# First stage of a hybrid mLSTM / RG-LRU / MoE step: token tiles in single file, loads of SP in one order, constants on ScalarE's queue

## The reference

```python
xs = x_sample + grid_pos_embed(x_sample.shape[1], D_MODEL)[None]        # latent tokens only
mod_ctx = (silu(c_ctx) @ w_ada[l] + b_ada[l]).reshape(1, N_MOD, D_MODEL)
mod_lat = (silu(c) @ w_ada[l] + b_ada[l]).reshape(bs, N_MOD, D_MODEL)
sh1, sc1, g1, sh2, sc2, g2 = [mod[:, j][:, None, :] for j in range(N_MOD)]
hn = rmsnorm(x, lp['norm1']) * (1 + sc1) + sh1
z = (hn @ lp['w_in'])      # q, k, v, o, gates (16 columns), xr, gr
```

## Time and profile before

| | |
|---|---|
| median of 3 runs | 2114.51 us (2108.32 to 2136.52) |
| profiled execution, its own time | 2117.95 us |
| its span | 2116.2 us |
| first stage, from the start to the first work of the next | about 90 us |
| TensorE's mean granted clock | 0.967 of full |

### The profile page before, as it was taken

One profiled execution on the slowest core, in us unless ns is written; L12 is line 12 of the kernel. 1 busy time (PEld: TensorE's weight loads), 2 busy tenths in 40 slices (PEclk: granted clock), 3 DMA queues, 4 the chain that ended last, 5 costly groups with the idle time before them and its releaser, 6 DMA issues. The chain is left out here.

```text
span 2116.2 us, 31750 instructions
## 1 busy us (share of the span) xinstructions
PE 1920.4 (91%) x8869; PEld 1342.3 (63%) x8870; DVE 1268.5 (60%) x1853; ACT 1072.9 (51%) x1530; POOL 740.4 (35%) x761
## 2 busy tenths in 40 slices
PE   4787998999998997699999999999999999999980
PEld 2344444999896454566777766767767777676660
DVE  3376447432778699675666555555665666555556
ACT  3354545442234111556666656566666666666652
POOL 4211000000013044443556444346656653335350
PEclk9899999999999998799999999999999999999995
DMA  8732200332104224337967897866677888887854
GB/s 262 237 134 102 67 21 20 120 120 71 11 1 175 90 90 150 140 135 261 321 170 225 305 324 244 298 181 171 165 252 253 273 275 283 279 295 250 283 141 178
DMA packets 119099, 390.10 MB, mean 184 GB/s; under 512 B 28541, under 2 KB 53117, under 8 KB 94077
## 3 DMA queue, kind: packets, MB, share of 16 engines
q1 hardware_dynamic: 72908, 271.53, 35.0%
q0 software_dynamic: 45840, 117.76, 21.7%
q10 hardware_dynamic: 290, 0.02, 0.0%
HBM read 347.08 MB, written 80.41 MB: 202 GB/s over the span
## 5 line engine op out<-in xcount | busy, mean ns | idle before, releaser
L2083 DVE TENSOR_TENSOR wupl<-big,wuph 128x2048 fp32r<-128x2048 f32 x234 | 525.8, 2289 | 462.0 <-ACT wuph L2021 398.7
L2021 ACT ACTIVATE wuph<-big 128x2048 fp32r (+1 forms) x234 | 435.8, 1917 | 13.0 <-issue 8.5
L1946 PE MATMUL bank<-w,hT 128*128 (+1 forms) x920 | 414.0, 593 | 0.3 <-issue 0.3
L1925 PE MATMUL bank<-wuph,xTh 128*128 128x512 f32 x928 | 372.2, 401 | 12.1 <-DVE xTl L2092 11.5
L1925 PE MATMUL bank<-wuph,xTl 128*128 128x512 f32 x928 | 364.6, 393 | 0.0
L1925 PE MATMUL bank<-wupl,xTh 128*128 128x512 f32 x928 | 363.4, 392 | 0.0
L1859 POOL DMA_INDIRECT yacc_scratch<-y,idx_s x106 | 213.3, 2012 | 422.3 <-issue 381.5
L1946 PEld LDWEIGHTS bank<-w,hT 128*128 128x128 f32 x920 | 166.0, 190 | 165.6 <-issue 165.6
L2011 ACT ACTIVATE y<-bank 128x512 f32<-128x512 f32 x115 | 68.8, 598 | 296.6 <-PE bank L1946 227.0
L1925 PEld LDWEIGHTS bank<-wuph,xTh 128*128 128x128 f32 x928 | 175.8, 189 | 49.4 <-issue 15.9
L1925 PEld LDWEIGHTS bank<-wuph,xTl 128*128 128x128 f32 x928 | 174.6, 188 | 37.1
(11 more groups left out here) (358 smaller groups left out, 2690.3 us busy)
## 6 DMA issues: line engine op xcount, KB each, us to landing
big<-in_exp_w SPq DMA_DIRECT2D x128, 1024.0 KB
w<-in_exp_w SPq DMA_DIRECT2D x64, 1024.0 KB
wada<-in_w_ada POOLq DMA_DIRECT2D x16, 1024.0 KB, 6.2
wg<-in_w_in SPq DMA_DIRECT2D x14, 1024.0 KB, 5.4
wada<-in_w_ada SPq DMA_DIRECT2D x4, 2048.0 KB, 11.5
big<-in_w_in SPq DMA_DIRECT2D x8, 1024.0 KB, 5.4
x<-x_scratch SPq DMA_DIRECT2D x9, 512.0 KB
x_scratch<-x SPq DMA_DIRECT2D x9, 512.0 KB, 2.6
```

Source lines behind the costliest of these rows:

```text
L1925: mm = pe.matmul(b_up[j][:, :], x[:, k, :], w[:, :, k, :], start=(k == 0 and i == 0), stop=(k == KT - 1 and i == 2))
L1946: mm = pe.matmul(b_down[half][:, :], hT[:, i, :], w2[:, at, i, half * 512:(half + 1) * 512].rearrange("p s n -> p (s n)"), start=(i == 0), ...
L2021: act.activation(part13(wup[j][0], half), raw13(e % WSLOT, half), ACT.Copy).then_inc(w_high, 1)
L2083: dve.tensor_tensor(part13(wup[j][1], half), raw13(e % WSLOT, half), part13(wup[j][0], half).bitcast(F32), ALU.subtract).then_inc(w_low, 1)
```

## The change

The tile groups stay, but only as the groups of the load semaphores. The work goes tile by tile: ACT takes a root for each tile (`root(t)`, two tiles ahead of the turn), DVE a reciprocal for each tile inside `norm(t)`, and DVE's loop does `position(t + 2)` and then `norm(t)`. PE does `position(t + 3)` behind `turn(t)`. The sequence of turns and blocks is now 0, 1, block 0, 2, 3, 4, block 1, 5, 6, block 2, 7, 8, block 3. SP issues tiles and blocks in one list, `LOADS`. POOL keeps the tables, the small loads and the stores; `cst` moves to ACT's queue.

```diff
--- before.py
+++ after.py
@@ -221,7 +221,7 @@
         ss, rs = sb("ss1", [P, NT]), sb("rs1", [P, NT])
         s_ada = [sem(f"ld_ada{j}") for j in range(NA)]
         s_bada, s_x1, s_pos = sem("ld_bada"), sem("st_x1"), sem("ld_pos")
-        s_x = [sem(f"ld_x{j}") for j in range(NG)]
+        s_x = [sem(f"ld_x{j}") for j in range(4)]
         pick_set, pos_in, gate_sums = (sem(n) for n in ("pick_set", "pos_in", "gate_sums"))
         s_cc, s_cst, bd_zero = sem("ld_cc"), sem("ld_consts"), sem("bd_zeroed")
         ring_banks, pos_banks, gate_bank, col_banks = m.banks[0:4], m.banks[6:8], m.banks[4], [m.banks[5], m.banks[7]]
@@ -236,14 +236,15 @@
         small = small_loads(a, m)
         m.ld_all = 16 * (len(small) - 1)
 
-        TAKE = [[0, 1], [2, 3], [4, 5], [6, 7, 8]]
-        group = {t: g for g, tiles in enumerate(TAKE) for t in tiles}
         MODS = [0, 2, 1, 3]
         BY_ACT, BY_DVE = (0, 1, 4), (2, 3, 5, 6, 7)
-        seq = ([("turn", t) for t in TAKE[0]] + [("mod", 0)] + [("turn", t) for t in TAKE[1]] + [("mod", 1)] +
-               [("turn", t) for t in TAKE[2] + TAKE[3]] + [("mod", 2), ("mod", 3)])
-        AHEAD = {("start", 0): [1, 2], ("turn", 1): [3], ("mod", 0): [4], ("turn", 3): [5], ("mod", 1): [6], ("turn", 5): [7, 8]}
-        COLUMNS = {("turn", 3): [0], ("turn", 6): [1], ("mod", 3): [2, 3]}
+        GROUP = [[0, 1], [2, 3], [4, 5], [6, 7, 8]]
+        group = {t: g for g, tiles in enumerate(GROUP) for t in tiles}
+        LOADS = [("x", 0), ("x", 1), ("mod", 0), ("x", 2), ("x", 3), ("mod", 1), ("x", 4), ("x", 5), ("mod", 2), ("x", 6), ("x", 7),
+                 ("x", 8), ("mod", 3)]
+        seq = ([("turn", t) for t in (0, 1)] + [("mod", 0)] + [("turn", t) for t in (2, 3, 4)] + [("mod", 1)] +
+               [("turn", t) for t in (5, 6)] + [("mod", 2)] + [("turn", t) for t in (7, 8)] + [("mod", 3)])
+        COLUMNS = {("turn", 5): [0], ("turn", 6): [1], ("mod", 3): [2, 3]}
         jobs_before, n = {}, 0
         for item in seq:
             jobs_before[item] = n
@@ -255,7 +256,11 @@
 
         @block.sync
         def _(sp):
-            for j in range(NG):
+            for kind, j in LOADS:
+                if kind == "x":
+                    src = a["x_prompt"][0] if j == 0 else a["x_sample"][0, (j - 1) * P:j * P, :]
+                    sp.dma_start(x[j][:, :], src).then_inc(s_x[group[j]], 16)
+                    continue
                 if j >= NA:
                     sp.wait_ge(full, jobs_before["mod", j - NA] + 1)
                 g = MODS[j]
@@ -278,13 +283,9 @@
             pool.dma_start(posr, a["pos_row"]).then_inc(s_pos, 16)
             for b in range(2):
                 pool.dma_start(posc[64 * b:64 * b + 64, :], a["pos_col"]).then_inc(s_pos, 16)
-            for t in range(NT):
-                src = a["x_prompt"][0] if t == 0 else a["x_sample"][0, (t - 1) * P:t * P, :]
-                pool.dma_start(x[t][:, :], src).then_inc(s_x[group[t]], 16)
-                for dst, src in small[3 * t:3 * t + 3]:
-                    pool.dma_start(dst, src, allow_slow_non_contiguous=True).then_inc(s_cst if dst is small[0][0] else m.ld, 16)
-                if t == 0:
-                    pool.memset(m.bd[:, :, :, :, :], 0.0).then_inc(bd_zero, 1)
+            for dst, src in small[1:]:
+                pool.dma_start(dst, src, allow_slow_non_contiguous=True).then_inc(m.ld, 16)
+            pool.memset(m.bd[:, :, :, :, :], 0.0).then_inc(bd_zero, 1)
             pool.wait_ge(full, total - 1)
             for t in range(NT):
                 pool.wait_ge(x_pos, t + 1)
@@ -335,7 +336,7 @@
 
             pe.wait_ge(pick_set, 1)
             pe.wait_ge(s_pos, 48)
-            for t in AHEAD["start", 0]:
+            for t in (1, 2):
                 position(t)
             pe.wait_ge(silu_c, 1)
             pe.wait_ge(s_bada, 16)
@@ -344,8 +345,8 @@
                     modulation(t)
                 else:
                     turn(t)
-                for tt in AHEAD.get((kind, t), ()):
-                    position(tt)
+                    if t + 3 < NT:
+                        position(t + 3)
                 for j in COLUMNS.get((kind, t), ()):
                     columns(j)
 
@@ -365,20 +366,20 @@
             ring = Ring(act, ring_banks, full, free)
             act.dma_start(m.cc[:, 0, :], a["c_ctx"].rearrange("(p k) -> p k", k=KT)).then_inc(s_cc, 16)
             act.dma_start(m.cc[:, 1, :], a["c"][0].rearrange("(p k) -> p k", k=KT)).then_inc(s_cc, 16)
+            act.dma_start(small[0][0], small[0][1]).then_inc(s_cst, 16)
             act.dma_start(bada[:, :], a["b_ada"][:, 0:NG * 512]).then_inc(s_bada, 16)
             act.wait_ge(s_cc, 32)
             act.activation(cct[:, :, :], m.cc[:, :, :], ACT.Exp, scale=-1.0).then_inc(e_cc, 1)
             act.wait_ge(s_cst, 16)
 
-            def squares(g):
-                for t in TAKE[g]:
-                    act.wait_ge(x_pos, t + 1)
-                    if t >= 1:
-                        act.wait_ge(x_sq, t)
-                    act.activation(sq, x[t][:, :], ACT.Square, accum_out=ss[:, t:t + 1]).then_inc(x_sq, 1)
-                c = slice(TAKE[g][0], TAKE[g][-1] + 1)
-                act.wait_ge(x_sq, TAKE[g][-1] + 1)
-                act.activation(rs[:, c], ss[:, c], ACT.Sqrt, scale=1.0 / D, bias=m.epsc).then_inc(x_root, 1)
+            def root(t):
+
+                act.wait_ge(x_pos, t + 1)
+                if t >= 1:
+                    act.wait_ge(x_sq, t)
+                act.activation(sq, x[t][:, :], ACT.Square, accum_out=ss[:, t:t + 1]).then_inc(x_sq, 1)
+                act.wait_ge(x_sq, t + 1)
+                act.activation(rs[:, t:t + 1], ss[:, t:t + 1], ACT.Sqrt, scale=1.0 / D, bias=m.epsc).then_inc(x_root, 1)
 
             def modulate(k):
 
@@ -387,6 +388,8 @@
                                          scale=sc_col[:, k, s:s + 1], bias=sh_col[:, k, s:s + 1])
                 ins.then_inc(done_act, 1)
 
+            root(0)
+            root(1)
             for kind, t in seq:
                 if kind == "mod":
                     bank = ring.drain()
@@ -394,8 +397,8 @@
                     act.wait_ge(mod_row, t + 1)
                     ring.drained(act.activation(mrow[t][:, 256:512], bank[32:34, 0:256], ACT.Copy))
                 else:
-                    if t == TAKE[group[t]][0]:
-                        squares(group[t])
+                    if t + 2 < NT:
+                        root(t + 2)
                     for half in range(2):
                         bank = ring.drain()
                         ring.drained(act.activation(m.hnT[:, 4 * half:4 * half + 4, t * P:(t + 1) * P],
@@ -425,7 +428,7 @@
                             m.ident[0:16, 0:16].unsqueeze(2).to_broadcast([16, 16, 64])).then_inc(pick_set, 1)
 
             def position(t):
-                dve.wait_ge(s_x[group[t]], 16 * len(TAKE[group[t]]))
+                dve.wait_ge(s_x[group[t]], 16 * len(GROUP[group[t]]))
                 if t == 0:
                     dve.sem_inc(x_pos, 1)
                     return
@@ -436,6 +439,8 @@
                 dve.tensor_tensor(x[t][:, 512:1024], x[t][:, 512:1024], posc, ALU.add).then_inc(x_pos, 1)
 
             def norm(t):
+                dve.wait_ge(x_root, t + 1)
+                link(dve.reciprocal(rs[:, t:t + 1], rs[:, t:t + 1]))
                 if t >= 2:
                     dve.wait_ge(full, jobs_before["turn", t - 2] + 2)
                 dve.tensor_scalar(hn[t % 2][:, :], x[t][:, :], rs[:, t:t + 1], None, ALU.mult).then_inc(x_hn, 1)
@@ -457,14 +462,12 @@
                                             ALU.mult, ALU.add)
                 ins.then_inc(done_dve, 1)
 
-            for g, tiles in enumerate(TAKE):
-                for t in tiles:
-                    position(t)
-                c = slice(tiles[0], tiles[-1] + 1)
-                dve.wait_ge(x_root, g + 1)
-                link(dve.reciprocal(rs[:, c], rs[:, c]))
-                for t in tiles:
-                    norm(t)
+            position(0)
+            position(1)
+            for t in range(NT):
+                if t + 2 < NT:
+                    position(t + 2)
+                norm(t)
             dve.wait_ge(m.ld, m.ld_all)
             for half in range(2):
                 modulation_columns(half)
```

## The result

The changed kernel takes 2122.94 us (median of 20 runs, 2118.93 to 2136.5), the kernel before 2113.09 (20 runs, 2106.98 to 2136.52). The ratio is 1.0049, 95% interval 1.0035 to 1.0063: **about 10 us slower**, far inside 2% and clear of the noise: the interval is 0.14% to either side, much finer than the 2% that the prediction named as the limit. The forecast was a loss of 1.4 us.

What follows compares the result with a forecast made beforehand. It took the first stage's end to be paced by tile 3's landing, block 0 and tile 8's landing; 75.8 - 74.4 = +1.4 us makes the profiled 2117.95 into 2119.4, forecast median 2116, range 2103 to 2134.

Steps and rivals of the forecast that it cites:

- A, the landing of tile 3: First loads of the first stage: tile 3 lands at 19.3 us, at 316 GB/s, bounds 18.8 to 29.0.
- A to the end of block 0: DVE and PE waiting for each other from tile 3's landing at 19.3; block 0 ends at 34.2.
- Block 0 to B: Block 2 and tiles 6 to 8, issued from 34.3 behind block 0; tile 8 lands at 47.8.
- B to the end of block 3: From tile 8's landing at 47.8: block 1 ends at 57.3, block 2 at 68.9, block 3 at 75.8.
- DVE's scaling of tile 0: On DVE behind the position of tile 2, so waiting for tiles 2 and 3; done at 21.7.
- the earlier constants: Constants on ACT's queue land at 9 to 10 instead of 15.5; six us won, nothing comes of them.
- the 16.0 us at the end: Fixed chain from the last block's end to the next stage's first matmul, 16.0 us, untouched by the change.
- The first turn: PE's first turn in the stage, claimed near 22 and not 24.4.
- The wait for tiles 6 to 8: DVE idle about 8 us before adding tile 6, from near 40 to 47.8, released by a transfer.
- the one on the slow side: Rival: SP's queue no faster than before, first loads until 29.0, block 3 ends at 85.5, +11 us, 2126; chance 0.12.
- Faster transfers: Rival: data sooner than the rates, tile 3 at 17, four transfers in 11.5; -2.9 us, 2112; chance 0.22.
- That rival: ScalarE changes tables for each root: up to 22 us more on ACT, time near 2130; chance 0.01.

Runs made afterwards that it cites:

- the two halves of the change: Two kernels against the kernel before: new loads with the old group order, ratio 0.9987; new tile-by-tile order with the old loads, ratio 1.0035.
- Small late: The changed kernel with POOL's small loads behind the landing of tiles 2 and 3; ratio 1.0007 to the kernel before.
- tiles ahead: The changed kernel with tiles 6 to 8 requested ahead of block 2; ratio 1.0022 to the kernel before.
- groups, same loads: Old group order with new loads, tiles 6 to 8 ahead of block 2, small loads behind tiles 2 and 3; ratio 0.9989 to the kernel before.
- loads only: The new SP load list and constants on ACT's queue, with the old group order; ratio 0.9987 to the kernel before.
- added matmuls: The changed kernel with extra PE matmuls, results unused, where PE waits; ratio 1.0046 to the kernel before.
- all three repairs: The changed kernel with scaling before next position, tiles 6 to 8 ahead of block 2, small loads behind tiles 2 and 3; 2099.86 us, ratio 0.9911 to the kernel before.
- before, small late: The kernel before with POOL requesting its small loads behind the requests of the nine tiles; ratio 1.0000 to the kernel before.

## Why the prediction was right in kind and wrong in size

The order of events was right, the size was not: 1.4 us were forecast and 11.05 are in the trace, 9.8 in the medians. The range held it because it was 31 us wide, mostly for the spread of few runs. And a forecast of 1.4 us hardly has a sign: it was the rest of gains and losses several times as large (7.7 us lost and 3.8 won in the two halves of the change), so that its sign came out is partly luck. Two terms failed, the rate of the first loads and the price of PE's work behind a wait. Step by step, each difference of 85.45 - 75.8 = 9.65 us has its place:

- **A, the landing of tile 3: 23.3 instead of 19.3, +4.0.** The term failed by its rate. I took 316 GB/s from a stretch in which POOL's list spread the small loads between 512 KB tiles. The change bunches them ahead of A, and the rate to 23 us was 246. *Small late* shows it: A came at 17.35. I had counted the small loads by their bytes, 0.1 MB, and they cost 6 us here.
- **A to the end of block 0: 19.7 instead of 14.9, +4.8.** The step's chain was right (turn, position, addition, scaling, each behind the other), its prices were not: turns 1.94 and 1.97 for 1.73, positions twice 2.07 for 1.12, block 0 7.0 for 4.15, in all 5.2. The prices came from a PE that had just done two turns in a row; the change gives it one turn and then a wait. The durations are those that PE has at the lower level of its clock from 50 to 60 us, though the column does not show the level here (last section). I named the clock only as something outside the stage.
- **Block 0 to B: 12.65 instead of 13.6, -0.95.** The four transfers were issued and landed as priced:

```profile
wada<-in_w_ada SPq DMA_DIRECT2D x1, 2048.0 KB, 8.6
yT<-in_x_sample SPq DMA_DIRECT2D x3, 512.0 KB, 10.0
```

  From the issue to the last landing they took 12.6 us. The rows gave 13.5, and the fit of the Trainium skill ("DMA: Bandwidth & Descriptors", Anatomy of one DMA) gave an estimate of 10.4. The page states this fit for transfers issued from GpSimd, and these are SP's; the measurement is nearer to the rows.
- **B to the end of block 3: 29.8 instead of 28.0, +1.8.** Again the durations: block 1 took 6.0 us, turn 4 1.97, position 7 2.07, and the loss is 2.75 at the end of block 1. Behind it 0.96 came back, because turn 5 took 1.10 for 1.73 and turns 7 and 8 1.97 for 2.68.

The steps on the order held. DVE's scaling of tile 0 waited for tiles 2 and 3; the earlier constants, 5.2 us and not six, were worth nothing, since tile 1's position was done at 15.04 and DVE then stood idle for the 8.26 us; DVE was idle for 8 us before tile 6 and tile 4's scaling stood right behind; the 16.0 us at the end did not move. The first turn, forecast near 22, began at 25.73, later than the 24.38 before. The wait for tiles 6 to 8 was put on the path with its full length, and *tiles ahead* shows that half of it was.

Of the rivals, the one on the slow side named +11 us and 2126, near the measured time, but its mechanism did not happen: it wanted A at 29.0, and A came at 23.3. Of the 9.65 us that the forecast missed, 4.0 are its kind of delay. *Faster transfers* was wrong as the change stood; with the small loads out of the way it came true (330 GB/s, A at 17.35). ScalarE loaded its table for the roots once, at 11.64, and never again in the stage. (That rival's price was off too: 22 us on top of 2116 make 2138, not 2130.) What I had not listed as a rival, PE's longer durations inside the stage, is the largest single miss, 5.2 us up to block 0 alone.

## What to carry to other kernels

When a loop is changed from groups to single items, look at what stands ahead of each step on its engine: "prepare t+2, then finish t" makes the finished item wait for the load of a later one, and swapping the two was worth 15.9 us of a 75 us stage. Price a PE step that will follow a wait at the longer duration that the trace shows behind a wait, not at the one it had in a run of work. Count small strided loads by their packets, and put them behind what is awaited, but expect a gain only where the tiles are what is waited for: it was 6.8 us in the changed kernel and nothing in the kernel before. And a transfer that is moved behind another one inherits that one's wait.

## What was not expected of the hardware

- Matmuls of one form have two durations in this stage, 1.12 and 2.07 for a position, 1.10 and 1.97 for a turn of eight, 3.62 and up to 6.48 for a block. The granted clock of two stretches of the changed kernel (busy us and count of PE, PEld, DVE, ACT and POOL, then the granted clock, the DMA share and GB/s):

```profile
30.00:40.00 10.00, 7.89 (x30) 3.36 (x32) 4.19 (x8) 2.64 (x5) 0.00 (x0) 1.00 0.01 5
50.00:60.00 10.00, 2.56 (x10) 1.68 (x9) 2.21 (x4) 2.04 (x4) 0.00 (x0) 0.50 0.46 177
```

  From 50 to 60 us it is 0.50, 1.2 GHz, and the durations are the long ones. From 30 to 40 it reads 1.00 with the same long durations. So early in a run the durations told the level and the column did not; in the kernels here it reads 1.00 until the first short matmuls have come. Why is open.
- Tiles that come earlier can cost PE time: *groups, same loads* against *loads only*, 4.0 us later at block 3's end with tiles 2 and 3 there by 18.9 instead of 24.3, most of it in longer matmuls. By which rule PE's level falls and rises was not settled; *added matmuls* kept it busy and did not keep it up.
- In *loads only* DVE's two scalings took 3.09 us, and 1.42 in the earlier trace rows. POOL cleared a tile in the same time (1.83 us from 18.36), and it put off the first turn by 1.7 us against *groups, same loads*. The same meeting stands in *groups, same loads* (3.31 us), in *all three repairs* (one scaling 1.47 instead of 0.75) and in the kernel before, where a TENSOR_SCALAR of 128x16 beside the clearing took 1.95 us and 0.17 in the changed kernel, which clears later. An addition (TENSOR_TENSOR) beside the clearing in *before, small late* kept its 0.69. The clearing need not be the only cause: in that run the two scalings took 1.97 us while POOL only requested loads. No run was made to test either.
